# First block's attention: diagonals of the softmax factors on GpSimd, and a turn by matmul, for batches of 256 keys

## The reference, cut to what matters

```python
s = jnp.einsum('bqgrd,bkgd->bgrqk', q, k).astype(jnp.float32) * scale
p = masked_softmax(s, mask)                    # over the keys
o = jnp.einsum('bgrqk,bkgd->bqgrd', p, v)
# kind A (8 heads in 2 groups): gates * (compressed, selected, window), summed
# kind B (8 heads): a band of 128 keys, and a sink in the denominator
# kind C (8 heads, 96 wide): causal
```

## Time and profile before

| what | value |
|---|---|
| median of 3 runs (lowest, highest) | 3055.42 us (3053.09, 3055.64) |
| the profiled execution, its own time | 3053.0 us |
| its span, first to last instruction | 3051.2 us |
| attention of layer 1, of layer 2 (by L1373, first to last start) | 159 to 243 us, 678 to 762 us |
| busy over the whole span: PE, PEld, DVE, ACT, POOL | 85%, 62%, 69%, 36%, 20% |
| mean granted TensorE clock | 0.942 of 2.4 GHz |

### The profile page before, as it was taken

How to read it: one execution, slowest core, us unless ns; L and a number is a source line. 1 busy time by engine, 2 the same in 40 slices (tenths; PEclk the granted TensorE clock), 3 DMA queues, 4 the chain that set the end, 5 groups by cost and what they waited for, 6 DMA issues and landing times. The chain is left out here.

```text
span 3051.2 us, 35562 instructions
## 1 busy us (share of the span) xinstructions
PE 2593.2 (85%) x13090; PEld 1889.6 (62%) x13090; DVE 2112.5 (69%) x4115; ACT 1087.8 (36%) x1979; POOL 609.9 (20%) x573
## 2 busy tenths in 40 slices
PE   8999999998999899899877667668999887666666
PEld 7968997896899797797543222225888653222222
DVE  6467665657765655554899888866674789888876
ACT  4364444446444465444222111113654221112111
POOL 0000000000000000000345454440000254544442
PEclk9999999999999999999999888889999998888898
DMA  6423554541455333243999999997434799999997
GB/s 255 171 97 125 179 184 154 181 167 70 156 181 192 143 128 122 97 166 139 412 426 421 427 426 427 427 427 302 158 111 159 310 426 420 426 427 427 426 427 311
DMA packets 112493, 810.80 MB, mean 266 GB/s; under 512 B 12736, under 2 KB 12736, under 8 KB 14272
## 3 DMA queue, kind: packets, MB, share of 16 engines
q0 software_dynamic: 73728, 536.90, 41.9%
q1 hardware_dynamic: 38592, 271.63, 24.5%
HBM read 807.44 MB, written 1.05 MB: 265 GB/s over the span
## 5 line engine op out<-in xcount | busy, mean ns | idle before, releaser
L3501 PE MATMUL ps<-arena 128*128 128x512 f32 x912 | 521.4, 722 | 235.7 <-ACT arena L3397 233.6
L167 DVE TENSOR_TENSOR ring_low<-ring,parts 128x2048 fp32r<-128x2048 f32 x214 | 487.7, 2291 | 317.1 <-ACT parts L161 313.5
L480 PE MATMUL ps<-parts,parts 128*128 128x256 f32 x2528 | 570.4, 283 | 11.7 <-DVE ring_low L167 10.0
L3501 PEld LDWEIGHTS ps<-arena 128*128 128x128 f32 x912 | 200.9, 230 | 541.9 <-ACT arena L3397 316.1
L480 PE MATMUL ps<-parts,ring_low 128*128 128x256 f32 x1824 | 512.9, 281 | 0.0
L161 ACT ACTIVATE parts<-ring 128x2048 fp32r<-128x2048 f32 x214 | 406.6, 1913 | 270.2 <-PE ps L488 109.7
L488 PE MATMUL ps<-parts,parts 128*128 128x512 f32 x1344 | 439.3, 396 | 7.7 <-DVE ring_low L167 5.7
L480 PEld LDWEIGHTS ps<-parts,parts 128*128 128x128 f32 x2528 | 429.0, 189 | 14.2 <-issue 12.9
L3224 POOL DMA_INDIRECT arena<-in_experts,stage_index x276 | 320.1, 1160 | 527.3 <-PE ps L3501 237.1
L3501 PE MATMUL ps<-ring,arena 128*128 128x512 f32 x616 | 312.5, 644 | 110.1 <-ACT arena L3397 107.5
L3272 DVE CUSTOM_DVE_ANT_0 arena<-arena 128x1024 f32<-128x1024 f32 x276 | 333.6, 1226 | 96.2 <-DMA arena<-in_experts,stage_index 93.6
(11 more groups left out here) (504 smaller groups left out, 2977.2 us busy)
## 6 DMA issues: line engine op xcount, KB each, us to landing
ring<-in_stream SPq DMA_DIRECT2D x249, 1024.0 KB, 4.8
arena<-in_experts,stage_index POOLq DMA_INDIRECT x276, 23.1
ring<-in_experts,stage_index POOLq DMA_INDIRECT x236
gain_row<-in_gain_rows SPq DMA_DIRECT2D x4, 512.0 KB, 5.7
arena<-in_mem SPq DMA_DIRECT2D x2, 1024.0 KB, 4.8
arena<-in_stream SPq DMA_DIRECT2D x2, 1024.0 KB, 7.7
par<-in_params SPq DMA_DIRECT2D x4, 386.0 KB, 4.6
x<-in_x SPq DMA_DIRECT2D x1, 1024.0 KB, 4.8
```

What stands on the lines that cost most here:

```text
L167: dve.tensor_tensor(k.ring_low[v % SLOTS], whole, self.high_of(v).bitcast(F32), ALU.subtract).then_inc(self.ph.sem("chunk_split"), 1)
L480: last = pe.matmul(self.ps[:, 2 * pair + f // 2, (f % 2) * T:(f % 2 + 1) * T], w[:, f * P:(f + 1) * P], x[:, k, :], start=(k == 0 and i == ...
L3501: last = pe.matmul(k.ps[:, bank + n, :], diag[:, s % ROWS, :], rows[row_of[s]][:, D + n * BLK:D + (n + 1) * BLK], start=(s % SLOTS_PER_TOK ...
```

## The change

For the batches of 256 keys only:

- `scale(b)` on VectorE ends with the factor; the multiplication L1373 of the probabilities is gone.
- GpSimd makes four diagonal matrices of the factors, one for each head: one multiplication of 128 x 512 elements, the identity times the factors, both read with a repeated axis. It waits for the factors and for a free buffer (two buffers in the arena for batches 6 to 11, one in the tile `hT` for 17 and 19).
- `turn(b)` waits for the diagonals too and issues a matmul where there was a transpose: the unscaled probabilities are the stationary operand, as before, and the diagonal is the moving one in the place of the identity. What lands in PSUM is the turned and scaled probabilities.

Batches of 128 and of 15 keys stay as they are.

```diff
--- before.py
+++ after.py
@@ -893,6 +893,7 @@
         self.kvcT, a = k.at(a, 2, T)
         self.branch_high, _ = k.at_parts(a, CHUNK)
         self.values, a = k.at(a, MT, 8, HD)
+        self.diag, _ = k.at(a, 2, 4, P)
         self.cqkv, a = k.at(a, MT, 2, T)
         self.small, a = k.at(a, MT, 56)
         self.sgate, a = k.at(a, MT, 24)
@@ -925,6 +926,7 @@
         self.hid, self.hid2 = self.kvcT[:, 0, :], self.kvcT[:, 1, :]
 
         self.cT, b = k.in_hT(0, 4, T)
+        self.late_diag = k.in_hT(b, 4, P)[0]
         self.squares = k.in_hT(b, T)[0]
         self.t3, b = k.in_hT(b, MT, 8, 16)
         self.t4, b = k.in_hT(b, MT, 8, 16)
@@ -1139,6 +1141,12 @@
         def out_ps(b):
             return k.ps[:, 6, 0:T]
 
+        def diag_of(b):
+            return z.diag[:, b % 2] if b < 12 else z.late_diag
+
+        def by_diagonal(b):
+            return batches[b].n_keys == 2 * P
+
         def up_bank(i):
             return shared if i < 5 else spare
 
@@ -1172,6 +1180,11 @@
                 pool.sem_inc(ph.sem("queries_rotated"), 1)
                 pool.wait_ge(ph.sem("hidden_done"), 1)
                 pool.tensor_copy(z.kC[:, :, :, HD:96], bc(z.kpr.unsqueeze(2), [P, MT, 8, 32])).then_inc(ph.sem("keys_roped"), 1)
+                for b in filter(by_diagonal, range(nb)):
+                    pool.wait_ge(ph.sem("probs_scaled"), b + 1)
+                    pool.wait_ge(ph.sem("probs_turned"), b - 1)
+                    pool.tensor_tensor(diag_of(b), bc(k.ident[:].unsqueeze(1), [P, 4, P]), bc(sums[:, b, :].unsqueeze(2), [P, 4, P]), ALU.mult
+                                       ).then_inc(ph.sem("diagonals_made"), 1)
 
             @block.tensor
             def _(pe):
@@ -1192,13 +1205,19 @@
                 def turn(b):
                     bt = batches[b]
                     pe.wait_ge(ph.sem("probs_scaled"), b + 1)
+                    if by_diagonal(b):
+                        pe.wait_ge(ph.sem("diagonals_made"), sum(map(by_diagonal, range(b + 1))))
                     if b >= 1:
                         pe.wait_ge(ph.sem("probs_turned_copied"), b)
                     if b == 6:
                         pe.wait_ge(ph.sem("up_copied"), 5)
                     for i, (k0, n) in enumerate(bt.key_tiles):
                         for h in range(4):
-                            last = pe.transpose(k.ps[0:n, 4 + i, h * P:(h + 1) * P], probs[:, b % 3, h, k0:k0 + n], k.ident[:])
+                            out, p = k.ps[0:n, 4 + i, h * P:(h + 1) * P], probs[:, b % 3, h, k0:k0 + n]
+                            if by_diagonal(b):
+                                last = pe.matmul(out, p, diag_of(b)[:, h, :], start=True, stop=True)
+                            else:
+                                last = pe.transpose(out, p, k.ident[:])
                     last.then_inc(ph.sem("probs_turned"), 1)
 
                 def values(b):
@@ -1366,9 +1385,14 @@
                     s = sums[:, b, :]
                     if bt.sink is not None:
                         link(dve.tensor_tensor(s, s, nmax[:, b, :], ALU.add))
-                    link(dve.reciprocal(s, s))
+                    factor = dve.reciprocal(s, s)
                     if bt.coef is not None:
-                        link(dve.tensor_tensor(bt.per_group(s), bt.per_group(s), bt.coef, ALU.mult))
+                        link(factor)
+                        factor = dve.tensor_tensor(bt.per_group(s), bt.per_group(s), bt.coef, ALU.mult)
+                    if by_diagonal(b):
+                        factor.then_inc(ph.sem("probs_scaled"), 1)
+                        return
+                    link(factor)
                     p = probs[:, b % 3, :, 0:bt.n_keys]
                     dve.tensor_tensor(p, p, bc(s.unsqueeze(2), [P, 4, bt.n_keys]), ALU.mult).then_inc(ph.sem("probs_scaled"), 1)
 
```

## The result

The changed kernel takes **3060.5 us** in the median of 12 executions (3055.7 to 3065.5). The kernel before, measured again beside it, takes 3051.6 (12 executions, 3047.6 to 3055.6). The ratio is 1.0029, with a 95% interval of 1.0022 to 1.0037: 8.9 us slower, between 6.7 and 11.3. The forecast had the sign, but said 3071.5, 16.2 us on its own base; 3060.5 lies just under its low end of 3061. Part of that gap is the base: three runs of before gave the forecast 3055.4, and twelve give 3051.6. Against the measured base the forecast rise is still nearly twice the real one. The profiled execution took 3061.7 us (span 3059.9).

A forecast was written before the change was run, and what follows sets the result against it. Neither TensorE nor VectorE alone was taken as the limit, but the order of work between them. Layer terms 5.2 + 1.8 + 1.1 = 8.1 us, two layers 16.2, on 3055.4 gave 3071.5 us; range 3061 to 3079.

The forecast's parts named there:

- What the waits meant: Waits of 34.7 us for L1373: turns wait for an applied factor, after the change for a factor made into a diagonal.
- The turn, +0.92: Each turn of 256 keys: 16 records where there were 8, 0.115 us each, +0.92 us at the full clock.
- The diagonal: GpSimd's 128x512 multiplication: 1.27 us after a 0.15 us start, so +0.17 us from factor to turn.
- The walk through batches 6 to 11: Shifts followed turn by turn: VectorE's freed time lost waiting for TensorE, turn 11 +4.25 us, +5.17 after it.
- Turn 17 at the lower clock: Turn 17 in batches 17 to 19, TensorE at 1.2 GHz: sixteen records in place of eight, +1.8 us a layer.
- Turn 19, +1.1: Last turn of the phase, after an idle wait: +0.17 for the diagonal and +0.92 for the turn, +1.1 us.
- The sum: Whole attention: 5.2 + 1.8 + 1.1 = 8.1 us a layer, 16.2 us for two layers.
- The clock stays up: Rival, 12%: matmuls keep TensorE at 2.4 GHz in batches 17 to 19; +3.4 us a layer, 3062 us.
- the forecast's own sign of being wrong: Forecast called wrong if, among other signs, the granted clock in batches 17 to 19 is 1.0.
- VectorE's pace: Rival, 5%: VectorE's own round bounds batches 6 to 11, so 7 us a layer come off, 3041 us.
- a turn no dearer: Rival, 8%: matmuls keep the transpose's 0.115 us, so less than 1 us a layer stays, 3057 us.
- Contention: GpSimd and VectorE hold each other up: within the forecast; if diagonals are held, +1.7 us a layer, 3075 us.

The follow-up runs named there:

- Kernel 1: Kernel before, with turns of 256 keys as matmuls with the identity and VectorE still multiplying: 3061.1 us, ratio 1.0026 to before.
- kernel 5: Changed kernel, but turns transpose with the identity; diagonals are made and unused, factors not applied: 3047.4 us, ratio 0.9987 to before.

## Why the prediction was right about the sign and wrong about the size

- **What the waits meant: right.** The turn waits for a factor's application, and after the change for its diagonal. TensorE's waiting did not go: its rows before turns 6 to 8 still show 1.28, 0.90 and 0.96 us. One reading was off: the 1.46 us before turn 8 is from the row of the weight loads, and TensorE's own row has 1.06; no term of the sum used it.
- **The turn, +0.92: right.** Turns of 256 keys take 2.02 to 2.05 us. Turn 9 to turn 10 and turn 10 to turn 11, where TensorE has no idle time, are 4.13 us each; the forecast said 4.1. The Trainium skill, "TensorE: Matmul & The Clock Gate", Terms, has the transpose mode as 4 times faster for FP32. The same eight tiles took 1.09 us as transposes and 2.02 as matmuls here, so the measurement gives about twice.
- **The diagonal: the term was mis-sized.** 1.27 us was the line through GpSimd's operations of 32 and 256 elements; it took 1.04, and began 0.09 after the factor ended (193.06 + 0.16, then 193.31), not 0.15. From reciprocal to turn are 1.58 us, where there were 1.67 and the forecast had 1.84. Three turns wait for it, 3 x 0.26 = 0.8 us, and the head turn was 0.7 less late than forecast.
- **The walk through batches 6 to 11: right in its mechanism.** L1428 and L1432 wait for TensorE (1.74 and 2.98 us), the freed 1.2 us is lost in those waits, and from turn 9 on each turn adds its own length. Kernel 1 shows the longer turn by itself and gets the same, kernel 5 its absence (head turn 0.74 us early).
- **Turn 17 at the lower clock, the step that failed.** The forecast was "sixteen need 3.75 if all are slow [...] **+1.8**". It took the lower clock of one profile as a property of the stage. In the changed kernel the clock stayed up in 7 layers of 8; there turn 17 took 1.95 us, and the 0.9 us by which it is longer than its transposes at the full clock are hidden behind ScalarE's split, so the term measured 0, not 1.8. (Its own words, fourteen slow records and two fast ones, would have given 1.6.)
- **Turn 19, +1.1: right in its mechanism.** With the clock up, the changed kernel's tail is 28.99 against 28.19, +0.8: the turn is 0.93 us longer, and it starts 0.11 us sooner where the forecast had 0.17 later, the diagonal's size again.
- **What falls cost: not in the sum.** The tail rose from 29.16 (91.98 less 62.82, the means of eight layers) to 29.40 (96.67 less 67.27), by 0.24 and not by 2.9. Falls cost before 1.0 us a layer on the mean (29.16 less 28.19), and the changed kernel 0.4, 3.3 us in one layer of eight. So the rarer falls took 0.6 off the 0.8.
- **The sum.** A layer is 4.45 (67.27 less 62.82) + 0.24 = 4.7 us longer, where the forecast had 8.1: of the 3.4 missing, 2.7 are batches 17 and 19 and 0.7 the diagonals. Where the clock did fall in the changed kernel, with the scores of batch 19 as in the forecast's profile, the layer is 6.9 us longer (99.56 against 92.64), turn 17 takes 3.62 us where 3.7 was forecast, and the tail grew by 2.5 against 2.9. So the sum was nearly right for a fall that seldom came.
- **The rivals.** "The clock stays up", with 12% and 3062 us, is what happened in 7 layers of 8, and the forecast's own sign of being wrong, a clock of 1.0 in batches 17 to 19, was met. It had +3.4 us for a layer against the first profile, and 96.26 less 92.64 is 3.6. VectorE's pace is refuted by kernels 1 and 5, and a turn no dearer by its 16 records. Contention is there, but not at the operations with one input in PSUM: `out` and `mask` keep their 0.42. Two splits were held, as shown below. `mask` of batch 19 stood behind the first and ended, with its small operations, at 242.8 us, but ScalarE took up that batch's exponentials only at 243.35; nothing stood behind the second.

**What stays open** is why the falls became rarer. Over all runs the clock fell in 12 of 16 layers whose turn 17 was transposed and in 4 of 20 where it was matmuls; by the turns of 6 to 11 it is 12 of 20 transposed and 4 of 16 matmuls. The Trainium skill, "TensorE: Matmul & The Clock Gate", Part 4, says of a transpose that it doesn't count as busy in the same way, and that the full clock doesn't engage for it. The tally leans that way, though the turns of 6 to 11 ran at a granted 1.00 as transposes.

The places of the falls split the tally in two. Twelve of the 16 began within 0.4 us of the start of batch 19's scores, which is ahead of turn 17, so the form of that turn can't have decided them in their own layer. They came in 9 of 20 layers with transposes in turns 6 to 11 and in 3 of 16 with matmuls. The other four began with turn 18 or later. Of the 24 layers whose clock was still up at turn 17 they are 4 of 8 with it transposed and 0 of 16 with matmuls. That fits turn 17 keeping the later falls away, but it is read from the runs afterwards, on few layers, and no run tests it. Batches 12 to 16, whose turns are transposes in every kernel here, were not tried with matmuls. That the changed kernel falls less often is measured; the cause is only argued.

## What to carry to other kernels

The time of an elementwise pass on the path is not gained by folding it into a matmul if its replacement has the same way from factor to consumer and makes the consumer, here the float32 transpose, twice as long: read which work follows which, not the wait total. Where a chain waits for a large operation, halving it and letting the consumer begin with the first half moved the head turn 1.0 us forward in each layer, for 0.07 us more of VectorE a batch (the two halves take 1.29 together, the whole 1.22; 0.16 more had been expected); the whole kernel's gain by that edit alone, 1.7 us, is at the edge of what the times can tell. And a fall of the granted clock in one profile is a draw: look at the same stage in the second layer and in a second execution before a term of the sum is built on it.

## What the runs showed of the hardware that was not expected

- GpSimd multiplies 128x512 float32 elements with two repeated inputs in 1.04 us; the line through its 32 and 256 element rows gives 1.27. VectorE takes 0.69 for the same diagonal.
- GpSimd's diagonal holds VectorE's operations that have both inputs in SBUF. The timeline of the changed kernel's VectorE and GpSimd at batches 17 and 19:

```profile
239.19 1.96 DVE L1450 TENSOR_TENSOR ring_low<-ring,parts 128x1024 fp32r<-128x1024 f32 x1
...
245.90 1.97 DVE L1444 TENSOR_TENSOR parts<-arena,parts 128x1024 fp32r<-128x1024 f32 x1
...
249.89 1.22 DVE L1444 TENSOR_TENSOR parts<-arena,parts 128x1024 fp32r<-128x1024 f32 x1
```

```profile
239.03 1.04 POOL L1186 TENSOR_TENSOR hT<-ident,hT 128x512 f32<-128x512 f32 x1 [21.19 <-DVE hT L1388]
245.75 1.04 POOL L1186 TENSOR_TENSOR hT<-ident,hT 128x512 f32<-128x512 f32 x1 [5.68 <-DVE hT L1388]
```

  The two that meet a diagonal take 1.96 and 1.97 us, the third 1.22, and in the kernel before all four splits of these batches take 1.21 to 1.22. `out` with one input in PSUM kept 0.41 to 0.42 beside a diagonal. The Trainium skill, "SBUF — State Buffer", "Who interferes with whom", says that a VectorE instruction with two SBUF inputs contends with a GpSimd instruction that reads SBUF, and that one with at most one SBUF input doesn't, outside VectorE's modes with two ports. This trace agrees: +0.75 us at the one, nothing at the other. The forecast left those modes out; no operation here was seen to be held in one.
- The same program's clock falls at places up to 6 us apart (79.2 and 85.6 us from the first scores) from one execution to the next, and a layer with a fall is 0.3 to 1.7 us longer than without one in before (91.31 to 92.70 against an estimated 91.01, 62.82 plus 28.19) and 3.3 in the changed kernel.
